# Loads and splits moved ahead of a stage's border, and one more small matmul, in a two-stack transformer kernel

## The reference, cut to what matters

```python
a = rms_norm(h, attn_norm[i])
mix = concat(diff_attention(a @ ...), ssd_mixer(a @ ...), gla_mixer(a @ ...))
h = h + mix @ w_out[i]
f = rms_norm(h, ffn_norm[i])
h = h + (silu(f @ w_ffn_gate[i]) * (f @ w_ffn_up[i])) @ w_ffn_down[i]
h = h + sigmoid(h @ ple_w_gate[i]) * (p[i] @ ple_w_proj[i])        # "ple" below
```

```python
sh1, sc1, g1, sh2, sc2, g2 = split(silu(c) @ ada_w[i] + ada_b[i])   # the modulation
x = x + g1 * attention_i(rms_norm(x, gain[i, 0]) * (1 + sc1) + sh1)
x = x + g2 * swiglu(rms_norm(x, gain[i, 1]) * (1 + sc2) + sh2)
```

## Time and profile before

| | |
|---|---|
| median of 3 runs | 2336.46 us (2334.03 to 2341.03) |
| the profiled execution | 2342.8 us, of which 2341.0 us are the span from the first to the last instruction |
| mean granted TensorE clock | 0.979 |
| PE busy | 2185.9 us (93%) |
| DVE busy | 1598.4 us (68%) |
| ACT busy | 1092.3 us (47%) |
| moved by DMA | 436.40 MB, mean 186 GB/s |

### The profile page before, as it was taken

How to read it: one execution, slowest core, us unless ns; L and a number is a source line. 1 busy time by engine, 2 the same in 40 slices (tenths; PEclk the granted TensorE clock), 3 DMA queues, 4 the chain that set the end, 5 groups by cost and what they waited for, 6 DMA issues and landing times.

```text
span 2341.0 us, 44967 instructions
## 1 busy us (share of the span) xinstructions
PE 2185.9 (93%) x17588; PEld 2075.4 (89%) x17588; DVE 1598.4 (68%) x2655; ACT 1092.3 (47%) x1752; POOL 0.2 (0%) x4
## 2 busy tenths in 40 slices
PE   5889999998899999898999999999988999998998
PEld 4779899987798999898999888999887999897998
DVE  4676587756756877566778766778777854666554
ACT  3545444445454443455444455544465444555443
POOL 0000000000000000000000000000000000000000
PEclk8999999999999999999999999999999999999999
DMA  4464399934653998444599544699543965542664
GB/s 125 107 162 147 104 303 300 292 100 110 166 158 104 302 299 282 117 143 138 189 301 297 184 145 131 215 300 298 169 127 122 291 193 166 144 134 83 191 185 135
DMA packets 545379, 436.40 MB, mean 186 GB/s; under 512 B 27472, under 2 KB 470904, under 8 KB 545144
## 3 DMA queue, kind: packets, MB, share of 16 engines
q1 hardware_dynamic: 541904, 431.21, 60.5%
q10 hardware_dynamic: 3368, 3.71, 0.5%
HBM read 433.82 MB, written 1.05 MB: 186 GB/s over the span
## 4 chain that ended last, share of the span: by engine, by line
PE 80%; DVE 9%; ACT 5%; DMA 2%; DVEq 2%; issue 1%; SPq 1%; ACTq 1%
PE bank L644 12%; PE bank L646 12%; PE bank L645 12%; PE acc L644 7%; PE acc L646 7%; PE acc L645 7%; PE bank L788 3%; PE bank L1160 2%; PE bank L844 2%; ACT w_hi L1284 2%; DVE w_lo L1734 1%; PE bank L654 1%; PE bank L709 1%; PE bank L710 1%; PE bank L713 1%
## 5 line engine op out<-in xcount | busy, mean ns | idle before, releaser
L1284 ACT ACTIVATE w_hi<-wslot 128x1024 fp32r<-128x1024 f32 x590 | 610.5, 1054 | 534.2 <-PE acc L646 253.5
L644 PE MATMUL bank<-h_hi,w_hi 128*128 128x256 f32 x2784 | 792.5, 285 | 27.3 <-DVE w_lo L1734 10.6
L645 PE MATMUL bank<-h_lo,w_hi 128*128 128x256 f32 x2784 | 778.3, 280 | 0.0
L646 PE MATMUL bank<-h_hi,w_lo 128*128 128x256 f32 x2784 | 778.3, 280 | 0.0
L1734 DVE TENSOR_TENSOR w_lo<-wslot,w_hi 128x1024 fp32r<-128x1024 f32 x412 | 494.2, 1221 | 219.4 <-ACT w_hi L1284 218.8
L644 PEld LDWEIGHTS bank<-h_hi,w_hi 128*128 128x128 f32 x2784 | 525.7, 189 | 45.4 <-DVE w_lo L1728 14.1
L645 PEld LDWEIGHTS bank<-h_lo,w_hi 128*128 128x128 f32 x2784 | 529.1, 190 | 2.2 <-issue 1.7
L646 PEld LDWEIGHTS bank<-h_hi,w_lo 128*128 128x128 f32 x2784 | 526.5, 189 | 0.0
L644 PE MATMUL acc<-mid_hi,w_hi 128*128 128x256 f32 x1120 | 317.7, 284 | 7.8 <-DVE mid_lo L2279 4.6
L646 PE MATMUL acc<-mid_hi,w_lo 128*128 128x256 f32 x1120 | 312.6, 279 | 0.0
L645 PE MATMUL acc<-mid_lo,w_hi 128*128 128x256 f32 x1120 | 312.6, 279 | 0.0
(11 more groups left out here) (286 smaller groups left out, 2987.1 us busy)
## 6 DMA issues: line engine op xcount, KB each, us to landing
wslot<-in_ada_w_dram SPq DMA_DIRECT2D x192, 512.0 KB, 5.7
wslot<-in_ffn_w_gate_dram SPq DMA_DIRECT2D x88, 512.0 KB, 4.9
wslot<-in_ffn_w_up_dram SPq DMA_DIRECT2D x88, 512.0 KB, 5.4
wslot<-in_ffn_w_down_dram SPq DMA_DIRECT2D x88, 512.0 KB, 3.7
wslot<-in_w_in_dram SPq DMA_DIRECT2D x72, 512.0 KB, 4.8
wslot<-in_sb_w_in_dram SPq DMA_DIRECT2D x48, 512.0 KB, 4.5
wslot<-in_w_ffn_gate_dram SPq DMA_DIRECT2D x44, 512.0 KB, 4.7
wslot<-in_w_ffn_up_dram SPq DMA_DIRECT2D x44, 512.0 KB, 5.4
```

Source lines behind the costliest of these rows:

```text
L644: pe.matmul(dst, w_hi[:, w, cols], hi, start=start, stop=False, skip_group_check=True)
L645: pe.matmul(dst, w_hi[:, w, cols], lo, start=False, stop=False, skip_group_check=True)
L646: return pe.matmul(dst, w_lo[:, w, cols], hi, start=False, stop=stop, skip_group_check=True)
L1284: return act.activation(dst, src, ACT.Copy)
```

## The change

1. **Early loads.** The norm at each of the five borders is `early`. In the stack-2 ffn phases, SP issues the next attention's loads for slots 0 and 1 near the start of the ffn, behind its first two steps, and no longer behind the ffn. In the stack-1 ffn phases the four loads for ple (units 0 and 1 of the gate, and the projection's two) move from before the last two steps to the same place near the start. At the borders after ple the three loads stay where they were.
2. **Early splits.** ACT and DVE split the attention's first two units at the end of the ffn phase, ahead of the addition to `xT`, or inside the last rounds of ple, and not at the start of the norm.
3. **Squares in ple.** At the two borders after ple, ACT squares `xT` inside ple's rounds (pairs 0 and 1) and right behind them (2 and 3), ahead of the table load.
4. **The last modulation block, late.** At the borders at 1320 and 1671 us the last block's two last units on DVE, its sum on PE and its store on DVE move into the norm: on DVE behind the addition and the gains, ahead of the scaling; on PE behind the sum of squares, ahead of the clearing and the four unread matmuls. The attention's value projection waits for the store.
5. **One more matmul.** `ada_sum` gets an fp32 matmul of a constant with one column ahead of its four; its result is not read. It runs 48 times.

```diff
+        early = split == "att" and prior != "setup"
+        late = None
+        if early:
+            was = phases[-1][2] if prior == "ple" else phases[len(kinds) - 1 - kinds[::-1].index("ffn")][2]
+            was.update(att_at=dict(at), att=more["att"], att_layer=more["layer"])
+            if prior != "ple" and ada_blocks(was["ada"]) == ADA_STEPS:
+                late = was["ada"], was["start"]
+        phase("norm", counts, split=split, early=early, late=late, squared=prior == "ple", **more)
...
+            def first_load(kind, l, n, used):
+                w, _, offs = att_weights(kind, l)
+                need = used.get(f"slot{n}", 0) + 1
+                if kind == "swa" and n:
+                    kv_load(w, n, 0, need)
+                else:
+                    load(n, mix_slot(n), unit(w, KT, offs[n]), need)
...
-                    for n in range(3):
...
+                    for n in range(2 if ph["early"] and not ph["squared"] else 0, 3):
+                        first_load(ph["att"], ph["layer"], n, at)
...
                     two_steps([None, 2 * P], [0, P], [base[n] + n % 2 + n // 4 for n in range(6)], *block(0), a_base)
+                    if ph["stack"] == 1:
+                        ple_unit(0, ph["layer"], ph["next"])
+                        ple_unit(1, ph["layer"], ph["next"])
+                        for n in range(2):
+                            used = ph["next"].get(f"slot{SLOT_PROJ + n}", 0)
+                            load(SLOT_PROJ + n, wslot[:, SLOT_PROJ + n, :], a["ple_w_proj"][ph["layer"]][P * n:P * n + P, :], used + 1)
+                    elif ph["att"]:
+                        for n in range(2):
+                            first_load(ph["att"], ph["att_layer"], n, ph["att_at"])
...
                 pe.wait_ge(consts_ready, 1)
+                pe.matmul(B(3, 8, 9), C("halves"), C("ones", 0, 1), start=True, stop=True)
                 for m in range(ADA_SLOTS):
...
                     mm.then_inc(sem["sumsq"], 1)
+                    if ph["late"]:
+                        ada_sum(ph["late"][1], ADA_STEPS - 1)
                     clear_acc()
...
-                    if blocks == ADA_STEPS:
+                    if blocks == ADA_STEPS and ph["stack"] == 1:
                         ada_sum(at, blocks - 1)
...
+            def first_high(kind, n, at):
+                mix_high(n, n, unit_loads(at, kind, n, 0))
+
+            def square_pair(q, ready):
+                act.wait_ge(sem["x_ready"], ready)
+                act.activation(sqT[:, 2 * q:2 * q + 2, :], xT[:, 2 * q:2 * q + 2, :], ACT.Square).then_inc(sem["squares"], 1)
...
                         if m + 5 < KT:
                             ple_high(m + 5, at)
+                        if m in (5, 6):
+                            first_high(ph["att"], m - 5, ph["att_at"])
+                        if m in (3, 5):
+                            square_pair(m // 2 - 1, g("x_ready") + m // 2)
+                    for q in (2, 3):
+                        square_pair(q, g("x_ready") + q + 1)
...
+                    if ph["late"]:
+                        ada, start = ph["late"]
+                        for n in (2, 3):
+                            ada_unit(start, ada, ADA_STEPS - 1, n, True)
...
+                    if ph["late"]:
+                        ada_store(start, ada, ADA_STEPS - 1)
...
                         if m + 5 < KT:
                             ple_low(m + 5)
+                        if m >= 6:
+                            first_low(m - 6, ph["att_at"])
```

More of the change, by code:

```diff
@@ L191, in norm @@
             counts.update(w_high=1, **slots(SLOT_MIX + 1, [1]))
-        phase("norm", counts, split=split, **more)
+        prior, kinds = phases[-1][0], [kind for kind, _, _ in phases]
+        early = split == "att" and prior != "setup"
[6 more added lines that the diff above has]
+        phase("norm", counts, split=split, early=early, late=late, squared=prior == "ple", **more)
     def first_units(counts):
@@ L218, in ffn @@
         start = dict(at)
-        phase("ffn", counts, ada=ada, **more)
+        phase("ffn", counts, ada=ada, start=start, att=None, **more)
         add(gate=None if more["stack"] == 1 else (more["layer"], 5), last=("down_done", 0))
@@ L617, in _ @@
                     i = NF // 2 - 1
[L618 to L623, removed]
                     two_steps([(NF - 1) * P, None], [(NF - 2) * P, (NF - 1) * P],
@@ L1620, in _ @@
                     act.preload_act_table_set(LN_EXP)
-                    if ph["split"] == "att":
-                        for n in range(2):
-                            mix_high(n, n, unit_loads(at, ph["att"], n, 0))
+                    if ph["split"] == "att" and not ph["early"]:
+                        first_high(ph["att"], 0, at)
+                        first_high(ph["att"], 1, at)
                     if ph["split"] == "ffn":
                         high(1, 3, 16 * (g("slot1") + g("extra1") + 1))
[L1626 to L1629, removed]
+                    for q in range(0 if ph["squared"] else 4):
+                        square_pair(q, g("x_ready") - 3 + q)
                     act.wait_ge(sem["sumsq"], g("sumsq") + 1)
@@ L1684, in _ @@
                     step(NF - 1, 1, more=False)
-                    for m in range(2 if ph["stack"] == 1 else 0):
-                        ple_high(m, ph["next"])
+                    for n in range(2):
+                        if ph["stack"] == 1:
+                            ple_high(n, ph["next"])
+                        elif ph["att"]:
+                            first_high(ph["att"], n, ph["att_at"])
                 elif kind == "ple":
@@ L1729, in low_of, with first_low @@
                    .then_inc(slot_used[n], 1)
+            def first_low(n, at):
+                low_of(n, n, at.get(f"high{n}", 0) + 1)
             def low(n, part, count):
@@ L2180, in _ @@
                     w = gain_of(gain)
-                    if ph["split"] == "att":
-                        for n in range(2):
-                            low_of(n, n, g(f"high{n}") + 1)
+                    if ph["split"] == "att" and not ph["early"]:
+                        first_low(0, at)
+                        first_low(1, at)
+                    if ph["late"]:
+                        ada, start = ph["late"]
+                        for n in (2, 3):
+                            ada_unit(start, ada, ADA_STEPS - 1, n, True)
                     if ph["split"] == "ffn":
@@ L2293, in _ @@
                     for b in range(2):
-                        step(NF - 2 + b, b, NF // 2 - 1, more=b == 0, block=blocks == ADA_STEPS)
-                    for m in range(2 if ph["stack"] == 1 else 0):
-                        low(PLE_SLOTS[m], PLE_PARTS[m], ph["next"]["w_high"] + m + 1)
+                        step(NF - 2 + b, b, NF // 2 - 1, more=b == 0,
+                             block=blocks == ADA_STEPS and (b == 0 or ph["stack"] == 1))
+                    for n in range(2):
+                        if ph["stack"] == 1:
+                            low(PLE_SLOTS[n], PLE_PARTS[n], ph["next"]["w_high"] + n + 1)
+                        elif ph["att"]:
+                            first_low(n, ph["att_at"])
                 elif kind == "modulation":
                     n = ph["ada"]
-                    if ada_blocks(n) == ADA_STEPS:
+                    if n < DEPTH:
                         ada_store(ph["start"], n, ADA_STEPS - 1)
```

2 lines of the change are left out of this document (added).

## The result

| | kernel before | changed kernel |
|---|---|---|
| median of 8 and 8 runs | 2338.46 us | 2349.44 us |
| lowest to highest | 2331.48 to 2342.78 | 2332.57 to 2357.57 |
| ratio after/before | | 1.0051, 95% interval 1.0033 to 1.0069 |
| the profiled execution | 2342.8 us | 2332.57 us |

The change makes the kernel some 11 us slower (0.5%), where 2331 us and a range of 2311 to 2342 had been forecast. The first thing to notice is that the profiled execution of the changed kernel is its fastest: the profile is 10 us shorter than before's, the median 11 us longer. One profile does not stand for this kernel, and why that is so is part of the answer.

A forecast was written before the change was run, and what follows sets the result against it. PE bounds the kernel, busy 93% of the span, so edits pay only where it idles. Terms -6.35 - 6.5 - 1.0 - 0.2 - 1.0 + 0.5 + 10.3 = -4.2 us, plus -1.3 for pace, gave 2331 us; range 2311 to 2342.

The forecast's parts named there:

- Early splits and squares after ple: Borders at 499 and 964 us: root starts earlier, PE not idle, full clock; 6.5 and 6.35 us gained.
- The moved loads: Ffn phases: 1.0 us gained in stack 1 (end waits gone, start stalls about 2 us), 0.5 us lost in stack 2.
- Rival (c): Ffn starts: early loads stall PE, 4 us more per stack-1 and 1.5 per stack-2 phase; 12 us, 2343 us; chance 0.10.
- The added matmul: Modulation sums on PE: two more passes, 0.223 us, in 46 dense groups; 10.3 us lost.
- rival (a): Ffn phases with modulation: ten-pass groups always leave the fast pace, 12.8 us gained; 2315 us, down to 2309; chance 0.20.
- The borders at 1320 and 1671 us: Squares' sum earlier but late modulation work delays PE; 1.0 us gained in all, bounds 3 gained and 1 lost.
- the one at 1987 us: Border without modulation block: splits delay the addition 1.2 us, last down unit may land earlier; 0.2 us gained.
- one chance in seven of 3.9 and of 6.5 us: Two long slow-pace stretches, 887 and 1463 matmuls, might turn fast; entered as -1.3 us.
- the clock at the ple borders: Sign: at the two borders after ple the granted clock stays 1.00.
- the sum's new place at 1320 us with PE idle before it: Sign: at 1320 and 1671 us the sum stands between L1160 and L677, with PE idle before it.
- no wait at the ends near 450 and 915 us: Sign: PE's 2.1 and 2.9 us waits at the stack-1 ffn ends are gone.
- loads near an ffn's start hold PE for more than 2 us: Ffn starts: one of two conditions for calling the prediction wrong; the other was the pace settling.

The follow-up runs named there:

- e10: Kernel before with only the squares in ple and early splits at the two borders after ple, no added matmul or moved loads: 2322.66 us, ratio 0.9933.
- e3: The changed kernel run again, unaltered, for a second profile: 2346.05 us, ratio to before 1.0030.
- e4: Changed kernel with the early loads moved from behind the ffn's first two steps to ahead of its last two: 2331.04 us, ratio to before 0.9964.
- the four pairs: Four comparisons of kernels with the added matmul against the same kernels without it: -4.8, -3.8, -1.2 and +5.0 us.
- e11: e4 without the added matmul: 2326.01 us, ratio to before 0.9942.
- e13: e4 with the last modulation block's sum and store back at the end of the ffn, second measurement of that kernel: 2333.27 us, ratio to before 0.9967.
- e12: e10 with the added matmul: 2321.45 us, ratio to before 0.9920.

## Why the prediction was wrong, step by step

- **Early splits and squares after ple (-12.85 us): right.** e10 has 17 us, interval 10 to 21. The clock stays at 2.4 GHz through the sum, and the root starts at 961.50, 2.1 us behind the last update of `xT` (1.9 to 2.1 forecast). One step inside was wrong without harm: no pass ran early, since PE is dense with ple until 957.85; all 16 follow it in 3.5 us.
- **The moved loads (-1.0 + 0.5 us): this is the step that failed.** They cost 15 us (e3 against e4), some 5 in stack 1 and the larger part in stack 2. The prediction let PE need gate unit 3 "behind step 2's silu ... at 294.0", with "a slack of 3.0 us". But PE takes that unit before step 2's down projection and not behind it: it multiplies the gate and up units of the next step first. The first row below, of the kernel before, PE in order of time, is its first matmul, straight behind step 1's down projection; the second, DVE in order of time, holds the unit's split and the next one's:

```profile
291.98 0.28 PE L644 MATMUL bank<-h_hi,w_hi 128*128 128x256 f32 x1
```

```profile
290.20 2.44 DVE L1734 TENSOR_TENSOR w_lo<-wslot,w_hi 128x1024 fp32r<-128x1024 f32 x2
```

  The unit's split, the first of the two, ended at 291.4, so the slack was 0.56 us and not 3.0. Of the difference 2.0 us are PE's order (291.98 for 294.0), and 0.5 us is DVE, busy with the modulation until 290.2: copy and subtraction took 2.9 us from the landing and not 2.4. After the change it ends at 295.8, 4.4 us later, and PE comes 1.3 us earlier, so the wait is 5.2 us, not 2, and the 1.2 GHz stretch behind it, which the sum left out, adds up to 1.7 us, half of a stretch of 3.4 us. In stack 2 "within the slack" fell for the same reason: 2.3 to 2.8 us each. Rival (c) had the mechanism, 12 us of it, with a chance of 0.10.
- **The added matmul (+10.3 us): the price was right, the pace was missed.** Ten passes are there, and the group is 0.22 us longer. (The floor of about 25 ns that the Trainium skill, TensorE: Matmul & The Clock Gate, Back-to-back issue gap, gives for matmuls of up to 64 columns shows only between the first two passes of a group, 0.03 us; the other distances in the trace are 112 ns.) But by the four pairs something gives back 5 to 15 us, in the mean 11, and the pace is what the profiles show for it: rival (a), chance 0.20, named the effect and its size (12.8 us). It was wrong in one point: the group does not fix the fast pace, it holds the one it finds.
- **The borders at 1320 and 1671 us (-1.0 us): mis-sized.** From the end of the squares' sum (1314.07) to the first tile (1322.24) it took 8.2 us, not 6.4: the clearing and unread matmuls at 1.2 GHz. The prediction knew that this could happen and counted half of it. The late sum itself took 1.56 us (1315.65 to 1317.21) and not 1.2. All stack-2 borders together, with the one at 1987 us: 2 to 12 us lost (e11 against e10, e13 against e12), not 1.2 gained.
- **The sum.** -17 (ple borders), -1 (added matmul with its pace), +2 to +12 (stack-2 borders), +15 (early loads) is between 1 us gained and 9 lost, against 7 (e3) and 11 us measured. The large errors were the loads and the pace, of opposite sign, and perhaps the stack-2 borders; that the pace made good for part of the loads was luck. The range ended at 2342 us, inside rival (c), and had no room for the loads and the borders together. Two slips did no harm: one chance in seven of 3.9 and of 6.5 us is 1.5 us and not 1.3, and 13.00/117 = 0.111 us is too short, since such a count takes in matmuls under way at the edges of the stretch.

Of the signs that the prediction named, four came as told (the clock at the ple borders, ten passes, the sum's new place at 1320 us with PE idle before it, no wait at the ends near 450 and 915 us); "loads near an ffn's start hold PE for more than 2 us" was its condition for being wrong.

## What to carry to other kernels

To price a load that is moved ahead of others, find the first matmul that reads each delayed unit in the trace of the kernel before, and subtract the end of its split: that is the slack, and a wrong picture of the order on PE can turn 0.56 us of slack into 3.0. Work that is moved behind a border can bring PE's idle, and with it the 1.2 GHz level, to a place where more work pays for it. And where the executions of one kernel spread by 25 us, its profile may be the fastest of them: a second profile and medians on the same chip are needed before a difference of 10 us is explained.

## What was not expected of the hardware

The same stream of weight load and matmul runs at 113.3 or 117.8 ns from start to start at the full granted clock. A group of 8 or of 12 passes with one column between two stretches turned the pace over in 216 cases of 216; a group of 10 left the fast one in 368 of 368, and a slow one stayed slow in 14 of 25. What makes the two paces, no run shows. Nor does one show why ffn phases mostly begin fast and the last one, in fourteen profiles, was slow six times.
